# The short convolution of the heads in token-by-channel form: two partition-shifting transfers in place of transposes

## The chip, the cores and the metric

The kernel runs on one NeuronCore of a Trainium2 chip. The metric is the device time of one execution in microseconds (us). Three runs of the kernel before took 2152.03 to 2153.05 us, median 2152.1 us.

## The reference

The program is a three-layer network on 256 tokens of 2048 channels. Only the first layer matters here, and of it the attention branch. Its projection `h @ w_in` yields queries, keys and values (3 x 2048 columns), which go through a causal convolution over tokens with four taps per channel and through SiLU, before they are cut into 16 heads of 128 channels:

```python
qkv = jax.nn.silu(causal_depthwise_conv(qkv, w_conv_qkv[i]))   # frame t sees t-3..t, one weight per tap and channel
q, k, v = jnp.split(qkv, 3, axis=-1)
q, k, v = l2norm(heads(q)), l2norm(heads(k)), heads(v)
o_a = gated_delta_chunked(q, k, v, g_log, beta)
```

With x[t] the projection of token t and w0 to w3 the taps of a channel, the convolution gives w3 x[t] + w2 x[t-1] + w1 x[t-2] + w0 x[t-3]. A second convolution with 31 taps (the B branch), two attention blocks of a second network and several square projections follow.

## The kernel before

**Blocks.** All large products have the same shape: 256 tokens by 2048 inputs by 512 columns, called a block. Blocks 0 to 15 are the heads (for head h its 128 query, key, value and gate columns), blocks 16 to 31 the groups of the B branch, and 54 more follow. A block has 16 chunks of 128 input rows; each chunk is six matmuls of 512 columns (two token tiles, each three products: high weight by high input, low weight by high input, high weight by low input). The high part `w_hi` is a rounded copy of the raw weights made by ScalarE (line 436), the low part `w_lo` the difference, made by VectorE (line 443). Both engines work six chunks ahead of TensorE (`AHEAD = 6`), in buffers of eight chunks. The raw weights stand in four units of four chunks in `raw`; SyncE loads a unit of the next block when VectorE has taken the unit's last chunk (`load_heads`, four transfers of 256 KB for a unit, 16 for a block of 4 MB).

**Work beside the products.** The order on each engine is written out by hand. A block has 32 half steps, called `hs`, two for each chunk. At each half step the functions `keys_*` and `scores_*` put their own instructions between the pieces: VectorE makes one piece of `w_lo` after every odd half step, ScalarE one of `w_hi` ahead of every even one. Engines take their instructions strictly in this order. While block h+1 is multiplied, `keys_*` work on head h; `scores_*` work on head h-1 in the same block. So a head's keys are treated beside blocks 1 to 16, and its scores one block later.

**A head in `keys_*`.** At half step 0 ScalarE scales the finished sum in PSUM into `proj` (256 tokens over 128 partitions in two tiles, 512 columns; lines 530 and 531) and frees the PSUM pair. At 3 TensorE turns the query, key and value columns of `proj` into channel-by-token form in PSUM (six transposes, line 516). At 4 VectorE copies them to `conv_in` (lines 593, 594), which has three zero columns on the left. ScalarE does tap 0 at 5 (line 540), VectorE taps 1 to 3 at 7, 10 and 13 (nine instructions at line 599): in this form a tap is a shifted read along the row and its weight one number for each partition (`cw`, staged by GpSimd from `chan`). Tanh at 14 (line 544), SiLU at 16 (line 608), six transposes back at 19 (line 522), two copies to `tok` at 20 (lines 548, 549), squares at 21 (line 557). GpSimd then makes the norms (`rn`, `scal`, lines 574 to 583).

**A head in `scores_*`.** Scaling at half step 1, decay at 3 and 6, transposes of the scaled tiles at 6 (line 618), copies at 7, products of keys and queries at 9 (line 624), `ap` at 11 (line 675), stores of `ap` and `ex` to HBM at 16 from ScalarE's queue (lines 643, 644).

**Start.** `chan` is filled with channel vectors that are turned by TensorE in block 0, in eight tiles (`ROW_TILES`), two of which carry the short convolution's weights.

**Groups.** Beside blocks 17 to 32 run the 31 taps of the B branch, partly on GpSimd (line 1036, `acc_p`) with VectorE's part at line 1067. `b_buffers_pool` zeroes this stage's buffers, before the first head.

## Time and profile before

| | |
|---|---|
| median of the runs | 2152.1 us |
| the profiled execution | 2152.86 us |
| its span, first to last instruction | 2151.1 us |
| TensorE matmul busy | 2125.1 us, 99% |
| VectorE busy | 1483.1 us, 69% |
| ScalarE busy | 1240.9 us, 58% |
| GpSimd busy | 336.9 us, 16% |
| moved by DMA | 439.71 MB, mean 204 GB/s |
| granted TensorE clock, mean | 0.998 |

The page gives for each engine its busy time, then the chain of work that ended last, the costliest groups of instructions and the DMA queues. Matmuls are pipelined, so that a busy TensorE means that it was never without one, not that it was at its peak. The heads' stage is the part from about 48 to 445 us of the span; the questions about it are asked of ten blocks in its middle, from 103.72 to 350.79 us.

### The profile page before, as it was taken

What the parts mean: (1) busy time and instruction counts of PE and PEld (TensorE: products, weight loads), DVE (VectorE), ACT (ScalarE), POOL (GpSimd) and SP (SyncE); (2) the same over time, 40 slices, a digit from 0 to 9 for tenths busy, and PEclk for the clock granted to TensorE, in tenths of its full rate; (3) what the DMA queues carried; (4) which work ended last, traced back from release to release, by engine and by line L of the source; (5) the groups of instructions that cost most, each with busy time, mean ns of one, the idle gap of its engine ahead of it and who ended that gap; (6) DMA issues with size and microseconds to landing.
All of it is one profiled execution on the core that took longest, in us unless ns stands there. A gap on an engine that the chain in (4) does not pass through costs nothing.

```text
span 2151.1 us, 29138 instructions
## 1 busy us (share of the span) xinstructions
PE 2125.1 (99%) x10033; PEld 1759.0 (82%) x10033; DVE 1483.1 (69%) x2750; ACT 1240.9 (58%) x2396; POOL 336.9 (16%) x456
## 2 busy tenths in 40 slices
PE   8999999999999999999999999999999999999998
PEld 6888888888888888888888877887888888888886
DVE  5877777788999987568665564643666745456666
ACT  6666666677777864457455554553454555555543
POOL 2111111147665641010000000000000000000000
PEclk9999999999999999999999999999999999999999
DMA  8777666678877866575767655564565555554452
GB/s 261 202 205 213 197 191 201 191 216 255 240 207 215 227 205 214 196 260 187 265 249 242 233 203 195 191 195 155 198 239 194 186 192 189 185 172 139 157 212 101
DMA packets 430627, 439.71 MB, mean 204 GB/s; under 512 B 27424, under 2 KB 302112, under 8 KB 428336
## 3 DMA queue, kind: packets, MB, share of 16 engines
q1 hardware_dynamic: 412640, 380.78, 57.1%
q0 software_dynamic: 7744, 35.98, 5.0%
q10 hardware_dynamic: 10128, 21.50, 2.7%
q8 instruction: 62, 1.02, 0.2%
q14 instruction: 53, 0.43, 0.1%
HBM read 410.92 MB, written 27.28 MB: 204 GB/s over the span
## 4 chain that ended last, share of the span: by engine, by line
PE 89%; DVE 7%; issue 1%; ACT 1%; POOL 0%; DVEq 0%; POOLq 0%; ACTq 0%
PE pair L462 26%; PE pair L464 26%; PE pair L463 26%; DVE w_lo L443 3%; DVE QB L1067 2%; PE QA L1510 1%; PE RA L1526 1%; PE RA L624 1%; PE QB L1595 0%; PE RA L800 0%; PE RA L1752 0%; PE RB L1752 0%; POOL acc_p L1036 0%; PE pair L484 0%; PE pair L483 0%
## 5 line engine op out<-in xcount | busy, mean ns | idle before, releaser
L443 DVE TENSOR_TENSOR w_lo<-raw,w_hi 128x512 fp32r<-128x512 f32 x1368 | 921.8, 694 | 411.6 <-ACT w_hi L436 410.9
L436 ACT ACTIVATE w_hi<-raw 128x512 fp32r<-128x512 f32 x1368 | 828.3, 625 | 465.1 <-PE pair L464 458.1
L462 PE MATMUL pair<-w_hi,in_hi 128*128 128x512 f32 x2336 | 936.5, 401 | 3.0 <-DVE in_lo L1135 2.8
L464 PE MATMUL pair<-w_hi,in_lo 128*128 128x512 f32 x2336 | 911.9, 390 | 0.0
L463 PE MATMUL pair<-w_lo,in_hi 128*128 128x512 f32 x2336 | 910.6, 390 | 0.0
L464 PEld LDWEIGHTS pair<-w_hi,in_lo 128*128 128x128 f32 x2336 | 438.8, 188 | 93.6
L462 PEld LDWEIGHTS pair<-w_hi,in_hi 128*128 128x128 f32 x2336 | 439.3, 188 | 91.3 <-DVE in_lo L1135 3.3
L463 PEld LDWEIGHTS pair<-w_lo,in_hi 128*128 128x128 f32 x2336 | 439.7, 188 | 86.5 <-issue 1.0
L1036 POOL TENSOR_TENSOR acc_p<-acc_p,tap 128x256 f32<-128x256 f32 x160 | 184.4, 1152 | 38.5 <-ACT tap L1010 25.1
L1010 ACT ACTIVATE tap<-upad,cwl 128x256 f32<-128x256 f32 x192 | 96.9, 508 | 51.9 <-POOL acc_p L1036 51.0
L1067 DVE SCALAR_TENSOR_TENSOR QB<-upad,cwl,QB 128x256 f32<-128x256 f32 x272 | 120.0, 482 | 0.0
L599 DVE SCALAR_TENSOR_TENSOR conv<-conv_in,cw,conv 128x256 f32<-128x256 f32 x144 | 61.2, 481 | 7.4 <-ACT conv L540 7.4
L574 POOL TENSOR_TENSOR rn<-ssq,pool_eps 128x4 f32<-128x4 f32 x16 | 3.2, 201 | 335.6 <-ACT junk L557 335.6
L2139 POOL DMA_DIRECT2D ln_vec_a<-in_ln_g_dram x1 | 0.5, 533 | 350.5 <-DVE mo L1724 350.5
L462 PE MATMUL pair<-w_hi,mem_hi 128*128 128x512 f32 x128 | 52.0, 406 | 0.0
L462 PE MATMUL pair<-w_hi,oa_hi 128*128 128x512 f32 x128 | 50.8, 397 | 0.0
L462 PE MATMUL pair<-w_hi,ub_hi 128*128 128x512 f32 x128 | 50.8, 397 | 0.0
L464 PE MATMUL pair<-w_hi,mem_lo 128*128 128x512 f32 x128 | 50.0, 391 | 0.0
L464 PE MATMUL pair<-w_hi,ub_lo 128*128 128x512 f32 x128 | 49.9, 390 | 0.0
L463 PE MATMUL pair<-w_lo,mem_hi 128*128 128x512 f32 x128 | 49.9, 390 | 0.0
L463 PE MATMUL pair<-w_lo,oa_hi 128*128 128x512 f32 x128 | 49.8, 389 | 0.0
L464 PE MATMUL pair<-w_hi,oa_lo 128*128 128x512 f32 x128 | 49.8, 389 | 0.0
(440 smaller groups left out, 1902.8 us busy)
## 6 DMA issues: line engine op xcount, KB each, us to landing
raw<-in_w_in_dram SPq DMA_DIRECT2D x512, 256.0 KB, 3.9
raw<-in_w_in_dram SPq DMA_DIRECT2D x80, 1024.0 KB, 5.1
raw<-in_w_out_dram SPq DMA_DIRECT2D x48, 1024.0 KB, 5.0
raw<-in_w_kv_shared_dram SPq DMA_DIRECT2D x24, 1024.0 KB, 5.0
raw<-in_w_br_a_dram SPq DMA_DIRECT2D x16, 1024.0 KB, 5.2
raw<-in_w_br_b_dram SPq DMA_DIRECT2D x16, 1024.0 KB, 6.1
raw<-in_w_mem_kv_dram SPq DMA_DIRECT2D x16, 1024.0 KB, 4.9
raw<-in_w_ple_gate_dram SPq DMA_DIRECT2D x16, 1024.0 KB, 5.0
```

The lines of the kernel that those rows point to most:

```text
L436: act.activation(piece(blk, q)[0], raw[:, u, q % UK], ACT.Copy).then_inc(hi_ready[u], 1)
L443: dve.tensor_tensor(lo, raw[:, u, q % UK], hi.bitcast(F32), ALU.subtract).then_inc(lo_ready[u], 1)
L462: pe.matmul(o, xh, wh, start=(q == 0), stop=False)
L463: pe.matmul(o, xh, wl, start=False, stop=False)
L464: mm = pe.matmul(o, xl, wh, start=False, stop=(q == KC - 1))
L599: ins = dve.scalar_tensor_tensor(conv[:, c], conv_in[:, c, k:k + S], cw[:, k, c:c + 1], conv[:, c], ALU.mult, ALU.add)
L624: mm = pe.matmul(RA[:, tile * S:(tile + 1) * S], kq[:, 2], kq[:, 0:2].rearrange("p c n -> p (c n)"), start=True, stop=True)
L1010: act.activation(tap[:, n % 2], upad[:, par, k:k + S], ACT.Copy, scale=cwl[:, k:k + 1])\
L1036: pool.tensor_tensor(acc_p[:, :], tap[:, 0] if n == 1 else acc_p[:, :], tap[:, n % 2], ALU.add)\
L1067: dve.scalar_tensor_tensor(a, src, cwl[:, k:k + 1], a, ALU.mult, ALU.add).then_inc(long_tap[k % 2], 1)
L1510: mm = pe.matmul(QA[:, tile * P:(tile + 1) * P], probT[:, at + key * P:at + (key + 1) * P], v(key), start=(key == 0), stop=(key == n - 1))
L1526: mm = pe.matmul(RA[:, at:at + keys], q[:, tile * P:(tile + 1) * P], k[:, 0:keys], start=True, stop=True)
```

## The change

The convolution of a head stays in token-by-channel form. The taps become products of whole tiles of 128 partitions by 768 elements (two token tiles of 384 columns) with weights that are the same in all partitions. The sum is split as w3 x + w2 x1 + shift by two of (w1 x + w0 x1), where x1 is x shifted by one token. A shift by n tokens is a shift by n partitions, done by two transfers from SBUF to SBUF on ScalarE's queue: one of 128-n partitions for both tiles, and one of n partitions from the end of tile 0 to the head of tile 1. The weights of a head are loaded by SyncE as broadcast rows, 4 x 384 numbers into each of 128 partitions (768 KB), double buffered. The 12 transposes of a head, the two copies out of PSUM, the tap on ScalarE, the nine of VectorE and the two copies into `tok` are gone. GpSimd gets three instructions of 128 x 768 for each head. The half steps of `scores_*` move back by three to five, some waits of the B branch's start move (its buffers are zeroed after the last head, the first `bg` load waits for the last head's `tok`), and SyncE's loop over the heads is unrolled.

```diff
+    def taps_in_sp(sp, h, par):
+        sp.dma_start(wt[:, par], t["w_conv_qkv"][0].rearrange("k (c m) -> k c m", c=3)[:, :, bass.ds(h * P, P)].partition_broadcast(P))\
+          .then_inc(s[f"wt_in{par}"], 16)
+
+    def shift_act(act, to, src, n, done):
+        act.dma_start(to[n:P, :, :], src[0:P - n, :, 0:QKV]).then_inc(done, 16)
+        act.dma_start(to[0:n, 1], src[P - n:P, 0, 0:QKV]).then_inc(done, 16)
 
     def keys_act(act, h, par, hs):
         if hs == 0:
             act.wait_ge(psum_ready, h + 1 + BLK_A)
-            reach(act, s["qkv_cols"], h)
+            reach(act, s["one_in"], 32 * h)
             reach(act, s["z_gated"], h)
+            reach(act, s["taps_on_dve"], 4 * h - 3)
+            reach(act, s["taps_on_pool"], 3 * h - 2)
...
         if hs == 1:
             act.wait_ge(psum_free, BLK_A + h + 1)
...
+            shift_act(act, by_one, proj, 1, s["one_in"])
             act.activation(z_th[:, :, :], proj[:, :, 3 * P:4 * P], ACT.Tanh, scale=0.5).then_inc(s["z_tanh"], 1)
-        if hs == 5:
...
         if hs == 14:
-            act.wait_ge(tap_done, SHORT * h + SHORT)
-            act.activation(conv_th[:, :, :], conv[:, :, :], ACT.Tanh, scale=0.5).then_inc(s["conv_tanh"], 1)
-        if hs == 20:
...
-        if hs == 21:
+            act.wait_ge(s["taps_on_dve"], 4 * h + 3)
+            shift_act(act, by_two, qkv_old, 2, s["two_in"])
+        if hs == 24:
+            act.wait_ge(s["taps_on_dve"], 4 * h + 4)
+            reach(act, s["tok_ready"], h)
+            act.activation(qkv_th[:, :, :], qkv_sum[:, :, :], ACT.Tanh, scale=0.5).then_inc(s["conv_tanh"], 1)
+        if hs == 28:
             act.wait_ge(s["tok_ready"], h + 1)
...
     def keys_pool(pool, h, par):
+        pool.wait_ge(psum_free, BLK_A + h + 1)
+        pool.wait_ge(s[f"wt_in{par}"], 8 * h + (16 - 8 * par))
+        reach(pool, s["taps_on_dve"], 4 * h)
+        pool.tensor_tensor(qkv_new[:, :, :], proj[:, :, 0:QKV], weight(par, 3), ALU.mult).then_inc(s["taps_on_pool"], 1)
         reach(pool, s["decay_diff"], h - 1)
         reach(pool, s["tok_scaled"], h - 1)
...
+        pool.wait_ge(s["one_in"], 32 * h + 32)
+        pool.tensor_tensor(qkv_tap[:, :, :], by_one[:, :, :], weight(par, 2), ALU.mult).then_inc(s["taps_on_pool"], 1)
+        pool.wait_ge(s["taps_on_pool"], 3 * h + 2)
+        pool.tensor_tensor(qkv_new[:, :, :], qkv_new[:, :, :], qkv_tap[:, :, :], ALU.add).then_inc(s["taps_on_pool"], 1)
...
     def keys_dve(dve, h, par, hs):
-        if hs == 4:
...
-        if hs in (7, 10, 13):
...
+        if hs == 3:
+            dve.wait_ge(psum_free, BLK_A + h + 1)
+            dve.wait_ge(s[f"wt_in{par}"], 8 * h + (16 - 8 * par))
+            reach(dve, s["two_in"], 32 * h)
+            dve.tensor_tensor(qkv_old[:, :, :], proj[:, :, 0:QKV], weight(par, 1), ALU.mult).then_inc(s["taps_on_dve"], 1)
+        if hs == 11:
+            dve.wait_ge(s["one_in"], 32 * h + 32)
+            reach(dve, s["tok_ready"], h)
+            dve.tensor_tensor(qkv_sum[:, :, :], by_one[:, :, :], weight(par, 0), ALU.mult).then_inc(s["taps_on_dve"], 1)
         if hs == 12:
+            dve.wait_ge(s["taps_on_dve"], 4 * h + 2)
+            dve.tensor_tensor(qkv_old[:, :, :], qkv_old[:, :, :], qkv_sum[:, :, :], ALU.add).then_inc(s["taps_on_dve"], 1)
...
-        if hs == 16:
+        if hs == 23:
+            dve.wait_ge(s["two_in"], 32 * h + 32)
+            dve.wait_ge(s["taps_on_pool"], 3 * h + 3)
+            dve.wait_ge(s["taps_on_dve"], 4 * h + 3)
+            dve.tensor_tensor(qkv_sum[:, :, :], qkv_new[:, :, :], by_two[:, :, :], ALU.add).then_inc(s["taps_on_dve"], 1)
+        if hs == 26:
             dve.wait_ge(s["conv_tanh"], h + 1)
-            dve.scalar_tensor_tensor(conv[:, :, :], conv_th[:, :, :], 1.0, conv[:, :, :], ALU.add, ALU.mult)\
...
+            dve.scalar_tensor_tensor(tok[:, :, :, :].rearrange("p t c n -> p t (c n)"), qkv_th[:, :, :], 1.0, qkv_sum[:, :, :],
+                                     ALU.add, ALU.mult).then_inc(s["tok_ready"], 1)
...
     def group_sp(sp, j):
+        if j == 0:
+            sp.wait_ge(s["tok_ready"], HEADS)
...
-        with sp.Fori(2, HEADS) as h:
+        for h in range(2):
+            taps_in_sp(sp, h, h)
+        for h in range(2, HEADS):
             load_heads(sp, BLK_A + h, COL_A, h)
+            sp.wait_ge(s["taps_on_dve"], 4 * h - 6)
+            sp.wait_ge(s["taps_on_pool"], 3 * h - 4)
+            taps_in_sp(sp, h, h % 2)
```

In `scores_*` the scaling goes from half step 1 to 6, the transposes from 6 to 10, the copies from 7 to 11, the products from 9 to 13, `ap` from 11 to 15 and the stores from 16 to 19.

## Rows read from the trace of the kernel before

**Rows 1.** The chain that ended last, in time: start us, us, what; two neighbouring blocks

```profile
103.72 0.86 PE RA L624 x4
128.43 0.86 PE RA L624 x4
```

**Rows 2.** Ten blocks: length; PE, PEld, DVE, ACT, POOL busy (instructions); clock, DMA share, GB/s

```profile
103.72:350.79 247.07, 247.07 (x1182) 206.03 (x1181) 193.42 (x431) 161.77 (x360) 32.81 (x80) 1.00 0.69 199
```

**Rows 3.** Who VectorE waited for in these ten blocks: total us, times, longest

```profile
DVE w_lo L443 <- ACT w_hi L436: 40.1, 30, 3.2
```

**Rows 4.** TensorE's instructions in time around six transposes: start us, us

```profile
61.63 0.39 PE L464 MATMUL pair<-w_hi,in_lo 128*128 128x512 f32 x1
61.86 0.49 PE L522 MATMUL QA<-const,conv 128*128 128x128 f32 x3
...
62.75 0.40 PE L463 MATMUL pair<-w_lo,in_hi 128*128 128x512 f32 x1
62.98 0.39 PE L464 MATMUL pair<-w_hi,in_lo 128*128 128x512 f32 x1
```

**Rows 5.** VectorE's groups in the ten blocks: count, busy us, mean ns, idle before

```profile
L599 DVE SCALAR_TENSOR_TENSOR conv<-conv_in,cw,conv 128x256 f32<-128x256 f32 x90 | 38.2, 481 | 4.4 <-ACT conv L540 4.4
L608 DVE SCALAR_TENSOR_TENSOR conv<-conv_th,conv 128x768 f32<-128x768 f32 x10 | 9.5, 953 | 0.0
L593 DVE COPY conv_in<-QA 128x512 f32<-128x512 f32 x10 | 6.9, 693 | 2.1 <-PE QB L516 2.1
L675 DVE TENSOR_TENSOR ap<-RA,dexp 128x512 f32<-128x512 f32 x10 | 6.9, 686 | 0.0
L594 DVE COPY conv_in<-QB 128x256 f32<-128x256 f32 x10 | 4.1, 415 | 0.0
```

**Rows 6.** VectorE in time: three taps, then two pieces

```profile
224.91 1.28 DVE L599 SCALAR_TENSOR_TENSOR conv<-conv_in,cw,conv 128x256 f32<-128x256 f32 x3 [0.45 <-ACT conv L540]
226.10 1.29 DVE L443 TENSOR_TENSOR w_lo<-raw,w_hi 128x512 fp32r<-128x512 f32 x2
```

**Rows 7.** GpSimd's instructions in time: small one in the heads, the groups' sum alone and twice

```profile
213.22 0.20 POOL L574 TENSOR_TENSOR rn<-ssq,pool_eps 128x4 f32<-128x4 f32 x1 [21.15 <-ACT junk L557]
...
454.72 0.74 POOL L1036 TENSOR_TENSOR acc_p<-acc_p,tap 128x256 f32<-128x256 f32 x1 [0.69 <-ACT tap L1010]
...
576.40 2.38 POOL L1036 TENSOR_TENSOR acc_p<-acc_p,tap 128x256 f32<-128x256 f32 x2 [0.16 <-POOL acc_p L1036]
```

**Rows 8.** VectorE in the same stretch: two pieces beside the second of these sums

```profile
577.34 1.98 DVE L443 TENSOR_TENSOR w_lo<-raw,w_hi 128x512 fp32r<-128x512 f32 x2
```

**Rows 9.** ScalarE's groups in the ten blocks: those that the change removes

```profile
L540 ACT ACTIVATE conv<-conv_in,cw 128x256 f32<-128x256 f32 x30 | 13.1, 500 | 8.9 <-DVE conv_in L594 8.9
...
L548 ACT ACTIVATE tok<-QA 128x384 f32<-128x384 f32 x10 | 4.9, 491 | 13.2 <-PE QB L522 13.2
```

**Rows 10.** Queues and issues in the ten blocks: packets, MB, share of 16 engines; us to landing

```profile
q1 hardware_dynamic: 84477, 41.95, 61.9%
q10 hardware_dynamic: 2880, 7.21, 7.3%
values_of_heads<-ex ACTq DMA_DIRECT2D x10, 448.0 KB, 6.0
scores_of_heads<-ap ACTq DMA_DIRECT2D x10, 256.0 KB, 4.6
```

**Rows 11.** ScalarE in time: the two evictions of a head and the tanh after them

```profile
219.13 0.69 ACT L530 ACTIVATE proj<-pair,small 128x512 f32<-128x512 f32 x1 [0.73 <-PE pair L464]
220.43 0.42 ACT L534 ACTIVATE z_th<-proj 128x256 f32<-128x256 f32 x1
```

**Rows 12.** Two issues of the whole execution: KB each, median us to landing

```profile
conv_and_gate<-ubz ACTq DMA_DIRECT2D x16, 256.0 KB, 2.2
bg<-in_b_gate_dram SPq DMA_DIRECT2D x16, 64.0 KB, 4.3
```

**Rows 13.** One of ScalarE's issues of a block, in time: start us, us

```profile
206.72 0.33 ACTq L643 DMA_DIRECT2D scores_of_heads<-ap  x1
```

128 lines of the change are left out of this document (53 added, 75 removed).

## The prediction

> **What bounds the kernel now.** I read the chain of waits first. In the heads' stage it is all TensorE, and the same matmuls come back after 24.71 us [rows 1]: the period of a block. The busy times of ten blocks agree: TensorE 247.07 of 247.07 us at a granted clock of 1.00, the higher of its two levels; VectorE 193.42, 19.3 us a block; ScalarE 161.77, 16.2 a block; GpSimd 3.3 a block; DMA at 0.69 of its sixteen engines [rows 2]. VectorE idles 5.4 us a block, of which 4.0 us is waiting for ScalarE's high pieces [rows 3], which wait for free buffers. So the stage is TensorE's, with VectorE next (78%) and the DMA engines at 69%, and six chunks of lead between the pieces and the matmuls. Whatever goes from TensorE here shortens the block, until something else needs more than what is left. The change touches 16 blocks, those in which a head's keys are treated; the rest of the time stays.
>
> **What goes from TensorE.** Twelve transposes a head. Around six of them the last matmul before starts at 61.63 and the second after at 62.75 [rows 4]: 1.12 us, where two steps of 0.23 would be 0.45. So six cost 0.67 us, twelve 1.33 us, and TensorE alone would need 24.71 - 1.33 = 23.4 us a block; over 16 blocks 21.3 us less. Clock and matmuls stay as they are.
>
> **VectorE.** Gone: two copies, 0.69 and 0.42 us [rows 5], about 0.95 with their overlap, and nine taps, of which three take 1.19 us from start to next start [rows 6], so 3.6 us. Added: four products or sums of 128 x 768. SiLU has that shape and takes 0.95 us [rows 5], 0.87 without the overlap: 3.5 us. SiLU stays. 19.3 - 4.55 + 3.5 = 18.3 us a block.
>
> **GpSimd.** Added: three sums or products of 128 x 768. The trace has 0.20 us for 4 elements and 0.74 us for 256, both with two inputs [rows 7]; the line through them gives 1.84 us for 768 (bounds 0.95, VectorE's time, and 3 x 0.74 = 2.2). Three are 5.5 us. GpSimd has the room, but it does not work beside VectorE for nothing: where a sum on GpSimd runs beside two pieces of `w_lo`, two sums take 2.38 us instead of 1.48 [rows 7] and the two pieces 1.98 us instead of 1.29 [rows 8, 6]. One waits for the other. So each of the three may hold VectorE for up to 1.84 us when its next instruction reads two tiles of SBUF (pieces, taps, SiLU): 0 to 5.5 us a block. The Trainium skill ("SBUF — State Buffer", section "SBUF: two separate sides") has this as an exclusive lock held for a whole instruction, between a GpSimd instruction and a VectorE one with two SBUF inputs; the trace agrees, with the 0.69 us that the two pieces lose.
>
> **ScalarE.** Gone: three taps (13.1 us in ten blocks) and two copies to `tok` (4.9 us for one of them [rows 9]), together 2.3 us a block; added: four issues. It stays below 16 us, and is hidden.
>
> **The transfers, in engine time.** In the ten blocks (3953 us of engine time over sixteen) the load queue took 61.9% for 84477 packets, 29 ns each at a mean of 497 bytes, and ScalarE's queue 7.3% for 2880, 100 ns each at 2504 bytes [rows 10]. By the line through these two a packet of 1536 bytes (384 columns) takes 66 ns. Per block and engine today: loads 15.3 us, stores 1.8 us. The weight rows add 1536 packets of 512 bytes, 96 an engine: 2.8 us. The first shift is 127 partitions by two tiles, 254 packets; the second 252; the small transfers of one and two partitions are negligible.
>
> **How many engines carry a shift** decides the case, and no row shows it: each transfer of the hardware queues in the profile has 128, 32 or 16 rows. Bounds: all sixteen take an equal share (16 x 66 ns = 1.05 us of engine time each), or one engine takes all: 254 x 66 ns = 16.8 us. I take one engine for the first shift, because 127 rows have no equal division but 1 and 127; the second shift's 126 rows divide by 14, so 18 packets or 1.2 us each. Then that one engine has 15.3 + 1.8 + 2.8 + 16.8 + 1.2 = 37.9 us of work a block, where the block now takes 24.7. And since every weight load has a sixteenth part on each engine, the loads cannot go round it.
> The Trainium skill ("DMA: Bandwidth & Descriptors", section "Why a DMA increments its semaphore by 16 and not by 1") states such a rule: a DMA runs on the largest number up to 16 that divides the slowest dimension of both sides, so 127 partitions on one engine. No run here shows it yet; with it the sum would be the one below, without it that of the first rival.
>
> **The path through a block, with one engine.** From the end of the block's matmuls:
> - evictions until the next instruction, 1.3 us [rows 11], then the shift is issued;
> - fixed time of a transfer: one of 256 KB lands after 2.2 us [rows 12], of which 16 KB an engine at 2504 bytes in 100 ns are 0.65: 1.5 us;
> - the 254 packets, 16.8 us;
> - loads on the same engine in between: each unit has 128 packets there, 3.7 us. One unit or two fall into this time, by packets in turn at most about as many as the shift's own, so 3.7 to 7.4 us, 10.2 with the weight rows. I take 7.4, since the engine has work left over from the block before (37.9 us).
> `one_in` is reached at 27.0 us. Queued behind this wait on VectorE (half step 11) are the pieces from chunk 11 on, so TensorE stands still after chunk 10, at about 15 us. After the wait: a product 0.87, then a piece 0.6; TensorE needs 6 x 0.227 = 1.36 us for each of the chunks 11 to 15 [rows 4] and 0.9 for the scores' products [rows 1]: 9.2 us if nothing else holds it. The sum at half step 12 (0.87), `zs` (0.42, like a copy of 256 elements), `ap` (0.69) [rows 5] and four more pieces lie beside that. GpSimd's second product is released by the same semaphore, and its sum follows at once: up to 2 x 1.84 us in which VectorE stands, and late pieces then cost TensorE up to 4.2 us. So 9.2 to 13.4 us; I take 12, near the upper end since both engines start together. Period: 27.0 + 12.0 = 39.0 us, which is above the engine's own 37.9 us, so both hold.
>
> The second shift (`two_in`, awaited at half step 23) is issued after the sum at half step 12 and needs 3 to 5 us; behind it are pieces of the next block, for which TensorE has not yet come. It is late next, if the first shift were not. SyncE waits for the taps of two heads before, and its queue holds `load_heads` of the next head behind that; these taps are long done, so nothing. Unrolling its loop: nothing.
>
> **Around the stage.** Two tiles less in `ROW_TILES` spare two small transposes and copies in block 0, some 0.5 us. The first `bg` waits for the last `tok` (half step 26) and then lands in 4.3 us [rows 12], about when half step 0 of the next block wants it: 0 to 2 us once, inside the six chunks of lead. I put the sum of these at nothing, bounds -1 and +3.
>
> **Sum.** 16 x (39.0 - 24.7) = 229 us. The profiled execution took 2152.9 us (span 2151.1), 0.8 above the median of 2152.1: 2152.9 + 229 - 0.8 = 2381 us.
>
> **Rivals.**
> - *The shift is spread over all sixteen engines* (the other side). Then a shift of 390 KB lands like the 448 KB store, in 6.0 us [rows 10]: `one_in` at 7.3 us, wanted at half step 11 or 8.0 us; `two_in` at 16.3, wanted at 16.8. DMA work is 15.3 + 1.8 + 2.8 + 2.1 = 22.0 us of 23.4, nearly full. TensorE's 23.4 us against VectorE's 18.3 + up to 5.5 = 23.8: period 23.4 to 24.1, 16 x -1.3 to -0.6 us: 2131 to 2143, say 2137 us. It decides from about five engines on: with 16.8/5 = 3.4 us `one_in` comes at 8 us. For it: only the even spread of all that the profile shows. Against it: 127. Chance 0.10.
> - *Spread, but VectorE and full DMA engines take the gain back.* VectorE's locks at their upper end (3 x 2.2) give 18.3 + 6.6 = 24.9 us a block, waits for late shifts a little more: 2150 to 2165 us. Chance 0.04.
> - *One engine, and ScalarE is held too.* For it: nothing in the rows; they have the 0.33 us that an issue takes now, with packets spread evenly [rows 13]. Chance 0.06.
> - Forecast, one engine: 0.80.
>
> **How the numbers follow.** Forecast's own bounds: the path with 3.7 us of loads between and no locks is 32.5 us, but the engine's own work keeps it at 34 at least even with packets a tenth cheaper: 2301 us. With 10.2 us between and 13.4 after, 43.2 us: 2449 us. The range reaches to the third rival: 2300 to 2480, which leaves out the spread cases (0.14) and a little. What a measurement of this kernel can tell from no change is about 0.2%, 4 us. Faster 0.10, same 0.02, slower 0.88.
>
> **What would show it.** In the profile after: blocks of 36 to 43 us in the heads' stage and unchanged ones behind; VectorE idle before the product of `qkv_sum` and GpSimd before that of `qkv_tap`, some 10 us a block, ended by a DMA; the shift's issue landing after 20 us and more, that of the second after 3 to 6; mean DMA share in the stage below 0.6 although more is moved. Wrong would be: landings of 6 us and blocks under 24.7 us (first rival); ScalarE's issues several us long (last). If the engine count is right and the size wrong, the terms to look at are the loads between the packets and the 12 us after the wait.

## The result, and the profile after

| | median, us | runs from to | ratio to before, 95% interval |
|---|---|---|---|
| before | 2152.1 | | |
| after | 2587.6 | 2584.0 to 2591.3 | 1.2023 [1.2007, 1.2039] |

Predicted were 2381 us, with a range of 2300 to 2480. The change costs 435 us, where I had 229. The stage is the one predicted, the size is not: a block of the heads' stage takes more than twice its former time. The profiled execution has a span of 2583.8 us and a mean granted TensorE clock of 0.913. Over the whole run TensorE is busy 2142.7 us against 2125.1: it has hardly more to do, it waits.

The chain of waits on the page of after, shares of the span by engine:

```profile
PE 59%; DMA 22%; DVE 10%; issue 3%; ACT 3%; ACTq 2%; POOL 0%; DVEq 0%; POOLq 0%
```

A transfer, which had no share in the chain before, now has 22%. The same chain in order of time, one block of after (start us, us, what), where the chain of before held TensorE alone [rows 1]:

```profile
524.97 0.72 ACTq L526
525.69 0.03 issue
525.72 36.15 DMA by_one<-proj
...
565.02 2.61 DVE qkv_old L608
567.65 0.83 ACTq L526
...
568.51 3.85 DMA by_two<-qkv_old
...
579.14 0.72 ACTq L526
...
579.89 33.45 DMA by_one<-proj
```

The first shift takes 36 us, the second 4, and 17 us lie between the first's landing and the next head's issue. The period is 54.2 us; over the stage, from the first issue at 48.2 to the sixteenth at 839.7, it is 52.8 us on average, against 24.7 [rows 1]. Fifteen times the difference are 421 of the 435 us.

Windows of after: thirteen blocks, one block, and the stretch in it in which TensorE stands (columns as in [rows 2]):

```profile
145.00:823.00 678.00, 332.04 (x1378) 272.13 (x1378) 278.88 (x469) 175.16 (x403) 115.59 (x131) 0.73 0.51 125
523.70:577.50 53.80, 24.04 (x103) 19.71 (x103) 21.08 (x37) 13.08 (x32) 8.56 (x11) 0.71 0.54 120
532.00:560.00 28.00, 0.90 (x4) 0.91 (x5) 6.02 (x18) 3.43 (x7) 0.00 (x0) 0.50 0.38 88
```

TensorE's work in a block is 24.0 us (23.4 were expected), in a block of 53.8. While it stands, the granted clock falls to 0.50, its lower level. The DMA engines carry 125 GB/s where they carried 199 [rows 2]. Nothing is busy: everybody waits. Who waits for whom in these thirteen blocks of after (total us, times, longest):

```profile
POOL qkv_tap L574 <- DMA by_one<-proj: 458.9, 14, 34.9
DVE z L595 <- ACT z_th L545: 354.3, 13, 29.9
PE RA L633 <- DVE ex L672: 346.0, 13, 29.8
ACT z_th L545 <- issue: 343.5, 13, 29.1
```

Read from the bottom: ScalarE's tanh of z waits 26 us a block for nothing but ScalarE's own queue; VectorE's `z` waits for that tanh; the scaled rows of the scores stand behind `z` on VectorE, and TensorE's transposes wait for them. So TensorE stands not at the place I gave (a late piece behind `one_in`) but earlier, at the scores. What holds ScalarE is seen in the rows of the tile `by_one` (duration of an issue in ns, min/median/max):

```profile
L526 ACTq DMA_DIRECT2D by_one<-proj x16: 717/727/1324, 48.2 to 839.7; - x16
L527 ACTq DMA_DIRECT2D by_one<-proj x16: 9940/25228/31187, 49.5 to 840.4; - x16
```

The issue of the 127 rows is done in 0.7 us, against 0.33 for an evenly spread one [rows 13]. The next issue, of one row, takes 25 us in the median. And the weights land late (issues of these thirteen blocks: KB each, median us to landing):

```profile
raw<-in_w_in_dram SPq DMA_DIRECT2D x208, 256.0 KB, 4.1
wt<-in_w_conv_qkv_dram SPq DMA_DIRECT2D x13, 768.0 KB, 22.6
```

768 KB in 22.6 us are 35 GB/s. The single packets in the trace of after show what moves in that block, in bins of 4 us (the weights were issued at 519.6, the shift at 525.0):

```
from us | shift packets of 1536 B | packets of 512 B (weights and loads) | mean ns of one of 512 B
521     |  0                      | 1163                                 |  48
525     |  0                      |  318                                 | 166
529     |  0                      |  290                                 | 116
533     |  0                      |  340                                 |  39
537     |  0                      |  463                                 |  82
541     | 43                      | 1656                                 |  31
545     | 48                      |  155                                 |  27
549     | 47                      |   46                                 |  27
553     | 57                      |   21                                 |  27
557     | 58                      | 1870                                 |  29
```

For 16 us after the shift's issue none of its packets moves; about 80 packets of 512 bytes a microsecond do at first, 41 GB/s. At about 541 the weights are in, the loads that had piled up pass (1656 packets in 4 us), and the shift's packets start, one each 75 ns or so, 65 ns of it its own time. They come one after another, all 254 of them, at least 60 ns apart; in the reordered kernel below, where the shift is cut at row 112, more than ten are under way at once. This is how one engine by itself would carry them.

### The profile page after: what moved, and what is told of

Its sections match the earlier page's. It is cut to its first block, busy times and chain, and to the rows that moved or that the text cites. A ratio compares the mean times of both kernels' runs of the same rounds, so it can differ in the third digit from the quotient of the medians.

```text
span 2583.8 us, 28297 instructions
## 1 busy us (share of the span) xinstructions
PE 2142.7 (83%) x9839; PEld 1766.9 (68%) x9839; DVE 1516.6 (59%) x2636; ACT 1197.7 (46%) x2316; POOL 426.8 (17%) x487
## 4 chain that ended last, share of the span: by engine, by line
PE 59%; DMA 22%; DVE 10%; issue 3%; ACT 3%; ACTq 2%; POOL 0%; DVEq 0%; POOLq 0%
DMA by_one<-proj 20%; PE pair L469 17%; PE pair L471 17%; PE pair L470 17%; DVE w_lo L450 3%; DMA by_two<-qkv_old 2%; DVE qkv_old L608 2%; DVE QB L1084 1%; ACTq L526 1%; ACTq L527 1%; ACT w_hi L443 1%; ACT junk L559 1%; PE QA L1530 1%; PE RA L1546 1%; DVE tok L623 1%
## 5 line engine op out<-in xcount | busy, mean ns | idle before, releaser
L450 DVE TENSOR_TENSOR w_lo<-raw,w_hi 128x512 fp32r<-128x512 f32 x1368 | 946.5, 711 | 362.6 <-ACT w_hi L443 360.5
L443 ACT ACTIVATE w_hi<-raw 128x512 fp32r<-128x512 f32 x1368 | 819.0, 625 | 515.7 <-PE pair L471 464.7
L633 PE MATMUL RA<-const,scaled 128*128 128x128 f32 x48 | 14.1, 429 | 385.9 <-DVE ex L672 385.9
L633 PEld LDWEIGHTS RA<-const,scaled 128*128 128x128 f32 x48 | 7.9, 208 | 392.6 <-DVE ex L672 225.5
L595 DVE SCALAR_TENSOR_TENSOR z<-z_th,proj 128x256 f32<-128x256 f32 x16 | 6.8, 425 | 429.7 <-ACT z_th L545 429.7
L545 ACT ACTIVATE z_th<-proj 128x256 f32<-128x256 f32 x16 | 6.7, 416 | 415.7 <-issue 415.7
L574 POOL TENSOR_TENSOR qkv_tap<-by_one,wt 128x768 f32<-128x768 f32 x16 | 41.5, 2594 | 495.0 <-DMA by_one<-proj 495.0
```

The costliest lines, as they stand in the source:

```text
L443: act.activation(piece(blk, q)[0], raw[:, u, q % UK], ACT.Copy).then_inc(hi_ready[u], 1)
L450: dve.tensor_tensor(lo, raw[:, u, q % UK], hi.bitcast(F32), ALU.subtract).then_inc(lo_ready[u], 1)
L574: pool.tensor_tensor(qkv_tap[:, :, :], by_one[:, :, :], weight(par, 2), ALU.mult).then_inc(s["taps_on_pool"], 1)
```

## The experiments

All on the changed kernel, with the kernel before on the same chip. The period is the average over the stage: from the first issue of `by_one` to the sixteenth, by fifteen.

| kernel | median, us | ratio to before, 95% interval | period, us |
|---|---|---|---|
| after | 2587.6 | 1.2023 [1.2007, 1.2039] | 52.8 |
| shift in 112 + 15 rows | 2375.2 | 1.1033 [1.1014, 1.1051] | 39.1 |
| two weight loads in all | 2380.4 | 1.1081 [1.1043, 1.1118] | 39.1 |
| small transfer first | 2635.1 | 1.2225 [1.2165, 1.2286] | 56.4 |
| 112 + 15 rows and two weight loads | 2273.6 | 1.0561 [1.0543, 1.0579] | 32.6 |
| 112 + 15 rows, distinct weight rows | 2252.2 | 1.0465 [1.0447, 1.0482] | 30.8 |
| 112 + 15 rows, weights by tap | 2387.9 | 1.1098 [1.1079, 1.1116] | 40.0 |
| scores later | 2271.4 | 1.0547 [1.0523, 1.0570] | 32.1 |
| distinct rows, narrow GpSimd | 2169.1 | 1.0082 [1.0065, 1.0099] | 25.7 |
| distinct rows, reordered | 2153.5 | 1.0005 [0.9996, 1.0015] | 24.6 |
| sixteen copies, reordered | 2181.2 | 1.0135 [1.0118, 1.0152] | 26.7 |
| the same, copies early | 2177.7 | 1.0110 [1.0093, 1.0126] | 26.5 |
| the same, shift in 127 rows | 2432.2 | 1.1300 [1.1281, 1.1319] | 42.2 |

### The shift cut at row 112

```diff
-        act.dma_start(to[n:P, :, :], src[0:P - n, :, 0:QKV]).then_inc(done, 16)
+        act.dma_start(to[n:n + 112, :, :], src[0:112, :, 0:QKV]).then_inc(done, 16)
+        act.dma_start(to[n + 112:P, :, :], src[112:P - n, :, 0:QKV]).then_inc(done, 16)
```

> The changed kernel with each large shift cut in two transfers of 112 rows (16 times 7) and of the 15 or 14 rows left, same bytes and same result; the small transfers stay. Theory A (127 rows ride on one DMA engine, and the weight rows' slow load, 20 us of packets on every engine, stands before them): the engine count no longer matters, the shift's packets take about 1 us an engine; if packets of the two queues take turns, one_in lands some 6 to 8 us after its issue and blocks come back after 24 us (about 2145 us); if the shift waits for the whole weight load, it lands after some 15 to 18 us and ScalarE's hold shrinks, blocks of 30 to 35 us (2240 to 2320 us). Theory B (a shift between partitions of SBUF is slow by itself, however it is spread): landing stays above 30 us, time stays near 2590 us.

Measured 2375.2 us: with the slow weight loads in place the one engine costs 212 of the 435 us, and 223 are left. The shift no longer needs 17 us of one engine, and still lands after 17.5 us (issues from 200 to 400 us: KB, us to landing):

```profile
wt<-in_w_conv_qkv_dram SPq DMA_DIRECT2D x5, 768.0 KB, 22.6
by_one<-proj ACTq DMA_DIRECT2D x5, 336.0 KB, 17.5
```

The weights land after 22.6 us here as in after, and the shift lands when they do. That is above the 2320 us at which the expectation ended: I had not thought that a spread shift would wait for the whole weight load.

### Weights for two heads only

```diff
-            taps_in_sp(sp, h, h % 2)
```

> The changed kernel without the weight loads of heads 2 to 15: these heads use the weight rows of heads 0 and 1, so that the load of 768 KB a head is left out; the shifts stay as they are. Theory A: the first packet of the shift comes 1.5 to 2 us after its issue instead of 15 to 16, the transfer of 254 packets lands after 19 to 25 us, ScalarE's second issue is held 10 to 16 us instead of 25 to 28; blocks of 36 to 40 us instead of 52, 2330 to 2400 us. Theory B, and a third one (C) by which the order of descriptors within ScalarE's queue and not the weight load delays the shift: no change, near 2590 us.

Measured 2380.4 us, as expected. Without loads of weights in its way the 127-row shift lands after 19 us (the chain in time), and the next issue is held 10 us instead of 25:

```profile
299.65 18.72 DMA by_one<-proj
...
336.66 19.00 DMA by_one<-proj
```

```profile
L527 ACTq DMA_DIRECT2D by_one<-proj x16: 10004/10690/34067, 49.5 to 634.8; - x16
```

So of the 25 us that ScalarE is held in after, about 15 are the time in which the weights block the shift, and 10 the one engine's. That this time is the predicted one is chance. The prediction had the weight rows in it, at 2.8 us, and two of its terms are off in opposite directions here: from TensorE's last matmul of a block to the landing it takes 21.4 us (334.28 to 355.66), where the prediction had 27.0, and from the landing to the block's last matmul 15.9 us (318.37 to 334.28), where it had 12.

### The small transfer first

```diff
-        act.dma_start(to[n:P, :, :], src[0:P - n, :, 0:QKV]).then_inc(done, 16)
         act.dma_start(to[0:n, 1], src[P - n:P, 0, 0:QKV]).then_inc(done, 16)
+        act.dma_start(to[n:P, :, :], src[0:P - n, :, 0:QKV]).then_inc(done, 16)
```

> The changed kernel with the two transfers of a shift issued in the other order, the one of one or two rows first; nothing else. Theory A (ScalarE is not held by the 127 rows' own issue but by the next issue behind it, until all but about a hundred of the 254 packets are through): ScalarE goes on at once, z_th and the high pieces follow, TensorE gets through chunk 10 instead of standing after chunk 4, while one_in comes as late as before (34 to 37 us after the issue). The block shrinks by the 6 chunks of 1.36 us and the 5 us from z_th to scaled, 52 to 41 or 45 us: 2410 to 2480 us. Rival (the hold is that of the large transfer's own issue, or TensorE waits for one_in anyway): 2570 to 2600 us.

Measured 2635.1 us, a miss on the wrong side. The held issue did go: ScalarE's two issues take 0.6 and 2.7 us in the median. But other instructions wait now, as long as before (waits from 200 to 400 us):

```profile
POOL qkv_tap L574 <- DMA by_one<-proj: 143.8, 4, 37.6
ACT w_hi L443 <- issue: 131.1, 8, 33.7
DVE qkv_sum L605 <- DMA by_one<-proj: 110.4, 4, 28.5
```

ScalarE's high pieces wait up to 33.7 us, but not for a held issue. In ScalarE's program the second shift's issue comes at half step 14, and ahead of it the wait for VectorE's sum, which needs the landed shift. The high pieces behind stand there too. One block in time, VectorE's sum and that issue, then the block's last matmul (the thirtieth after TensorE's stand, five chunks) and the eviction behind it:

```profile
330.62 2.58 DVE L608 TENSOR_TENSOR qkv_old<-qkv_old,qkv_sum 128x768 f32<-128x768 f32 x1
333.23 0.66 ACTq L526 DMA_DIRECT2D by_two<-qkv_old  x1
...
341.87 0.39 PE L471 MATMUL pair<-w_hi,in_lo 128*128 128x512 f32 x1
...
343.81 0.67 ACT L536 ACTIVATE proj<-pair,small 128x512 f32<-128x512 f32 x1
```

TensorE gets through chunk 10 before it stands, as expected, and has five chunks left at the landing (327.5) instead of eleven. It doesn't help, for two reasons. It comes out of a stand of 19.3 us at the lower clock level and needs 11.5 us for these five chunks. And the next head's shift is not issued when TensorE is through, but when the second shift (4.9 us), the last sum, SiLU and the squares are done, which stand ahead of the evictions in ScalarE's program: the eviction comes 1.5 us after the last matmul's end, 0.5 us in after. From the landing to the next shift's issue it takes 18.1 us here (272.40 to 290.52) and 17.3 in after. So the hold lies beside the wait for the shift and this chain: taking it away gives nothing while the shift takes 36 us. What makes the block 3.6 us longer than in after is not settled; the two landings shown by the chain take 38.0 and 36.4 us, against 36.2 and 33.5.

### Both: 112 + 15 rows, weights for two heads

> Both edits of the first two: shifts of 112 and 15 (14) rows, and no weight loads for heads 2 to 15 (these heads use the weights of heads 0 and 1). Theory A: what is left is the arithmetic of the change; one_in lands after 5 to 7 us, TensorE is never without work in the heads' stage or VectorE, locked by GpSimd's three instructions, is just as slow: blocks of 23.4 to 24.7 us, 2131 to 2152 us. If VectorE's and GpSimd's contention costs more than its measured durations say: 25 to 28 us a block, 2160 to 2205 us. Theory B: above 2500 us.

Measured 2273.6 us. A shift (its 336 KB) now lands after 3.1 us in the median, and 121 us over the kernel before remain, above both expectations. With the two runs before it makes a square:

| | weights each head | weights of two heads |
|---|---|---|
| shift in 127 rows | 2587.6 | 2380.4 |
| shift in 112 + 15 rows | 2375.2 | 2273.6 |

The weight loads cost 207 us beside the slow shift and 102 beside the fast one; the one engine costs 212 with the loads and 107 without. Together they cost more (314 us) than the two alone added up (209), though the landings nearly add (3.1, 17.5, 19 and 36 us): with a landing of 3.1 us the block of 32.6 us is bound by something else, and the first delay uses up part of that time. The third part, 121 us, is neither. About 21 of it are the weights of the first two heads, which are still loaded slowly (see the distinct rows below). The rest has its rows here, from the waits and from VectorE in time, 200 to 400 us:

```profile
PE RA L634 <- DVE ex L673: 34.1, 7, 5.0
DVE z L596 <- ACT z_th L546: 28.6, 7, 4.1
```

```profile
233.37 0.42 DVE L596 SCALAR_TENSOR_TENSOR z<-z_th,proj 128x256 f32<-128x256 f32 x1 [4.08 <-ACT z_th L546]
...
236.52 3.77 DVE L670 TENSOR_SCALAR scaled<-tok,scal 128x128 f32<-128x128 f32 x3
...
240.40 0.67 DVE L670 TENSOR_SCALAR scaled<-tok,scal 128x128 f32<-128x128 f32 x3
```

TensorE waits up to 5 us in each block for the scaled rows. Before these VectorE stands 4.1 us for the tanh of z, which is queued behind three issues on ScalarE (0.71, 0.91 and 0.61 us), and then three scalings take 3.77 us that take 0.67 elsewhere.

### Scores four half steps later

```diff
-        if hs == 10:
+        if hs == 14:
```

This is TensorE's wait for the scaled rows; likewise the copies, products and `ap`, and the tanh ahead of the issues; otherwise as the run before.

> The kernel of e4_both (even shifts, weight loads for heads 0 and 1 only) with two shifts of order: ScalarE does the gate's tanh before it issues the first shift, and the transposes, copies, products, ap and stores of scores_* come four half steps later on every engine. Theory F (in e4_both TensorE idles 5 us a block in front of the scores' transposes, because VectorE is late with scaled, and then runs some 4 us at the lower clock): both go, blocks of 23.4 to 25 us, 2135 to 2160 us. Rival G (VectorE and GpSimd are together full, and the idle time only moves to the pieces of w_lo): 2230 to 2275 us.

Measured 2271.4 us; it moved nothing (2273.6 before). The wait found another place: the copies of the scores, now at half step 15, stand on ScalarE behind half step 14, where it waits for VectorE's sum and then issues the second shift (waits, 200 to 400 us).

```profile
ACT kq L652 <- issue: 58.4, 7, 8.4
PE RA L640 <- ACT ex L653: 26.0, 7, 3.8
```

VectorE's three scalings still take 3.86 us beside GpSimd in this run, and its sum, which ScalarE waits for, comes behind them. The theory that the scores were only placed too early fell with this run. The time is in the range of its rival, that VectorE and GpSimd are together full, but the run leaves GpSimd's work as it is and can't show that.

### What makes the weight load slow: distinct rows

The same 1536 packets of 512 bytes to the same partitions, but each partition reads rows of its own of `w_in` and not all 128 the same 6 KB. Shift in 112 + 15 rows.

```diff
-        sp.dma_start(wt[:, par], t["w_conv_qkv"][0].rearrange("k (c m) -> k c m", c=3)[:, :, bass.ds(h * P, P)].partition_broadcast(P))\
+        sp.dma_start(wt[:, par].rearrange("p k c m -> p (k c) m"), w_in[:, 0, 0:12 * 1408].rearrange("p (g m) -> p g m", g=12)[:, :, bass.ds(h * 64, P)])\
```

> The kernel of e1_rows112 with another source for the weight rows: 1536 pieces of 512 bytes a head as before, but each partition reads twelve pieces of its own row of w_in instead of the same twelve pieces of w_conv_qkv as all others (so the taps are wrong numbers). Theory D (the weight load is slow, 23 us for 768 KB at 80 packets a us, because 128 partitions read the same 6 KB of HBM, and all other packets stand behind it): landing 4 to 8 us, shifts of 2.5 to 4 us, time near that of e4_both, 2270 to 2300 us. Theory E (it is slow by its size, its number of pieces or the shape of the access, whatever it reads): landing stays at 20 to 25 us and the time near e1_rows112's 2375 us.

Measured 2252.2 us, against 2375.2 with the broadcast. The landings (200 to 400 us):

```profile
wt<-in_w_in_dram SPq DMA_DIRECT2D x6, 768.0 KB, 6.1
by_one<-proj ACTq DMA_DIRECT2D x7, 336.0 KB, 3.1
```

22.6 us have become 6.1 for the same bytes, packets and destination, and the shift's 17.5 have become 3.1. So it is neither the volume nor the 512-byte packets. It is that one stretch of HBM is read by all partitions, and what ScalarE's queue has to move waits meanwhile. (The tensor read is another one too, but `w_conv_qkv` is not slow by itself: where distinct stretches of it are read, in the copying of the run with sixteen copies further down, 96 KB in pieces of 512 bytes land after 2.6 us.) The time is even 21 us below that of the kernel without loads: the first two heads' weights came sooner too (waits for them 19.8 us over all engines, 40.9 there).

### Weights in four transfers, one a tap

```diff
-        sp.dma_start(wt[:, par], t["w_conv_qkv"][0].rearrange("k (c m) -> k c m", c=3)[:, :, bass.ds(h * P, P)].partition_broadcast(P))\
+        for k in range(SHORT):
+            sp.dma_start(wt[:, par, k], t["w_conv_qkv"][0].rearrange("k (c m) -> k c m", c=3)[k, :, bass.ds(h * P, P)].partition_broadcast(P))\
```

> The kernel of e1_rows112 with the weight rows of a head in four transfers of 192 KB, one for each tap, instead of one of 768 KB; same bytes, same result. Theory D (same HBM bytes for all partitions): each of the four goes at the same slow rate, 5 to 6 us each, 20 us in all, and the shift of ScalarE's queue waits for those already handed over; 2340 to 2380 us. Theory E in its form 'the one large transfer keeps the others out until it has ended': the shift gets in between two of the four, lands after 4 to 9 us, 2290 to 2330 us.

Measured 2387.9 us, 13 us above the run with one transfer and 8 above the expected range. Four shorter transfers let nothing through between them: the shift still lands after 18.1 us in the median. The slow load is not a matter of the size of one transfer.

### GpSimd's three instructions made narrow

```diff
-        pool.tensor_tensor(qkv_tap[:, :, :], by_one[:, :, :], weight(par, 2), ALU.mult)
+        pool.tensor_tensor(qkv_tap[:, :, 0:4], by_one[:, :, 0:4], weight(par, 2)[:, :, 0:4], ALU.mult)
```

and likewise the other two, on the kernel with distinct rows.

> As the run with distinct weight rows (2252.2 us), and GpSimd's three instructions of a head work on 4 of their 768 columns only; so the current token and the token one back are left out of the sum, and the sum of the older two taps takes their place. GpSimd's 5 to 8 us of 768-column work per head, during which VectorE's instructions there were longer (3.8 us for the scaled rows against 2.1), are gone; VectorE's own work and all transfers stay. Theory G, what is left over the kernel before (100 us, 6.2 per block) is for the most part VectorE standing while GpSimd works: 3 to 5 us per block come back, 2170 to 2205 us, and the idle time of TensorE before the scores' transposes (79 us in the whole run) falls to under 40. Theory H, it is VectorE's own work and the wait for the shifts: GpSimd's instructions lie beside it and the time stays at 2235 to 2255 us.

Measured 2169.1 us, 83 us less than 2252.2, and 1 us below the range of the theory that VectorE stands for GpSimd. In the kernel with distinct rows, VectorE and GpSimd in time:

```profile
330.63 2.34 DVE L450 TENSOR_TENSOR w_lo<-raw,w_hi 128x512 fp32r<-128x512 f32 x1
332.89 2.02 DVE L687 TENSOR_TENSOR dexp<-dexp,const 128x256 f32<-128x256 f32 x1
334.84 0.68 DVE L450 TENSOR_TENSOR w_lo<-raw,w_hi 128x512 fp32r<-128x512 f32 x1
335.44 0.66 DVE L670 TENSOR_SCALAR scaled<-tok,scal 128x128 f32<-128x128 f32 x3
```

```profile
330.22 2.20 POOL L575 TENSOR_TENSOR qkv_tap<-by_one,wt 128x768 f32<-128x768 f32 x1 [1.79 <-DMA by_one<-proj]
332.50 2.13 POOL L577 TENSOR_TENSOR qkv_new<-qkv_new,qkv_tap 128x768 f32<-128x768 f32 x1
```

A piece of `w_lo` takes 2.34 us instead of 0.68, and `dexp` 2.02 instead of 0.42, each until 0.3 to 0.6 us after the end of a GpSimd instruction. Together they put the scaled rows 3.3 us later. The two instructions of GpSimd are released by `one_in`, so they come just then: the faster the shift, the earlier in the block they fall, ahead of the scores. This is why a shift of 3.1 us did not bring the time back.
With narrow instructions TensorE's wait for the scaled rows falls, and the clock stays at its higher level; the waits from 145 to 400 us, first with distinct rows, then with the narrow instructions:

```profile
PE RA L634 <- DVE ex L673: 44.8, 9, 5.0
```

```profile
PE RA L634 <- DVE ex L673: 17.4, 10, 1.8
```

From 145 to 640 us this idle time is 64.7 us with wide instructions and 20.7 with narrow ones, where the expectation said under 40. Over the whole profile TensorE's idle time falls by 52 us (108.8 to 56.6) and its busy time by 30 (2140.2 to 2110.4), for the same matmuls. The 30 go with the clock: with waits of 5 us a block its mean from 200 to 400 us is 0.89, with waits of 1.8 it is 1.00. The Trainium skill ("SBUF — State Buffer", section "SBUF: two separate sides") has the lock between GpSimd and a VectorE instruction with two SBUF inputs as one for the whole instruction; the 2.34 and 2.02 us agree with that. In the kernel with both edits the scalings, which have one input, took 3.77 us beside GpSimd.

### Reordered

Nothing left out but the true weights (distinct rows again). The tanh of z comes ahead of the first shift's issue, the issue moves to half step 4, and GpSimd waits for the scaled rows before its wide instructions:

```diff
+            act.activation(z_th[:, :, :], proj[:, :, 3 * P:4 * P], ACT.Tanh, scale=0.5).then_inc(s["z_tanh"], 1)
+        if hs == 4:
...
             shift_act(act, by_one, proj, 1, s["one_in"])
-            act.activation(z_th[:, :, :], proj[:, :, 3 * P:4 * P], ACT.Tanh, scale=0.5).then_inc(s["z_tanh"], 1)
...
         reach(pool, s["taps_on_dve"], 4 * h)
+        reach(pool, s["tok_scaled"], h)
         pool.tensor_tensor(qkv_new[:, :, :], proj[:, :, 0:QKV], weight(par, 3), ALU.mult).then_inc(s["taps_on_pool"], 1)
```

> As the run with distinct weight rows (2252.2 us), with three things moved and nothing left out: the gate's tanh runs ahead of the shift's issue in ScalarE's program, the first shift is issued three half steps later (after the half step's evictions), and GpSimd waits with its three 768-column instructions until VectorE has written the scaled rows of the scores before. Theory G (VectorE stands while GpSimd works): the scaled rows come 1.5 to 2 us sooner, TensorE's idle time before the scores' transposes falls from 79 us to under 50 in the whole run, and the time to 2190 to 2225 us. Theory H: 2240 to 2260 us, the later GpSimd work only puts the last sum later.

Measured 2153.5 us (2149.3 to 2157.1), no difference from before, and 99 us less than in the old order: more than I had expected of it. The three moves were made together, so the share of each is open. The window from 200 to 400 us, and TensorE's neighbours in the waits of that stretch:

```profile
200.00:400.00 200.00, 198.19 (x894) 162.24 (x893) 187.07 (x310) 117.49 (x263) 110.76 (x86) 1.00 0.94 273
```

```profile
POOL qkv_new L571 <- DVE ex L675: 47.2, 9, 5.2
DVE z L598 <- ACT z_th L541: 7.4, 9, 0.8
```

TensorE works all the time again, at the higher clock level, and the period in the middle of the stage is 23.9 us (GpSimd's first small sum starts at 318.57 and again at 342.43), below the 24.7 of before. GpSimd and VectorE lose no less to each other than they did, but where six chunks of lead cover it:

```profile
326.30 6.05 POOL L571 TENSOR_TENSOR qkv_new<-proj,wt 128x768 f32<-128x768 f32 x1 [5.24 <-DVE ex L675]
```

1.84 us of work take 6.05 here. VectorE is busy 187 of 200 us and the DMA engines 94%. So little more could come from the order: the block gains 0.8 us, about 12 us over the stage, which the first heads, whose weights are late, eat up (TensorE is busy 133.8 of the 140 us from 60 to 200, against 140.0 before).

### The whole computation with sixteen copies of the weights

```diff
+        for i in range(16):
+            sp.dma_start(taps_dram[i].rearrange("h (q m) -> h q m", m=P), t["w_conv_qkv"][0].rearrange("k (c h m) -> h (k c) m", c=3, m=P))\
+              .then_inc(s["out_stored"], 16)
...
-        sp.dma_start(wt[:, par], t["w_conv_qkv"][0].rearrange("k (c m) -> k c m", c=3)[:, :, bass.ds(h * P, P)].partition_broadcast(P))\
+        for g in range(P // 16):
+            sp.dma_start(wt[16 * g:16 * g + 16, par].rearrange("p k c m -> p (k c m)"), taps_dram[:, bass.ds(h, 1), :].rearrange("i a n -> i (a n)"))\
```

> The changed kernel whole, with nothing left out: shifts cut at row 112, the order of the run before, and the weights read in each head from sixteen copies in HBM that the kernel makes at its start (each of the 16 copies is read by 8 partitions in place of one 6 KB stretch by 128; 16 times 98 KB of copying ahead of the first head). Theory D, it is the 128 readers of one stretch that make the weight load slow: its landing falls from 22.7 us to under 12, and the time is that of the run before plus at most 20 us, 2200 to 2250 us. If eight readers of one stretch are slow too, the landing stays over 15 us and the time at 2300 to 2375 us.

Measured 2181.2 us, 406 us less than after, 1.35% above before, and below the expected 2200 to 2250 us. Each transfer of sixteen partitions lands after 4.3 us in the median, as the reading of the slow load wants it: eight readers of one stretch are not slow.

With the copies issued between the raw loads of the second block and the first head's weights ahead of the decays' transfers:

> As the run with sixteen copies (2181.2 us), nothing left out: the copies are issued one after each raw load of the second block (not in a row behind them), and the first head's weights ahead of the decays' two transfers. In the run before, the engines waited 43.6 us for the weights of the first two heads and TensorE was busy 120.4 of the 140 us from 60 to 200, against 133.8 in the run with distinct rows. Expected: those waits fall by 10 to 25 us, and with them the time to 2155 to 2172 us; the block of the ten middle heads stays. If it stays at 2178 to 2184 us, the first heads were not on the path.

Measured 2177.7 us (2172.2 to 2178.8), hardly less, a miss. The waits for the first weights did fall (from 43.6 to 23.7 us over all engines), but the middle of the stage got no better (window from 200 to 400 us):

```profile
200.00:400.00 200.00, 186.65 (x822) 153.13 (x821) 168.47 (x286) 106.95 (x245) 74.95 (x78) 0.97 0.95 256
```

The DMA engines are at 95% there, carrying 256 GB/s instead of the 273 of the reordered kernel. The shift lands after 4.8 us in place of 3.1. So 24 us over the reordered kernel stay; they go with the DMA engines, which are full in both, but that is argued and not shown; which property of the copied loads makes them dearer (6 KB in one piece, eight issues a head, eight readers) was not tried. No version that computes the whole beats the kernel before.

### The one engine by itself

The kernel of the run before, with the shifts in 127 and 126 rows again.

> As the run before of this call, with one thing put back: each shift again in 127 and 126 rows, so that the 127 rows of the first go to one engine. It is the price of the one engine alone, with the weights landing in about 5 us and GpSimd's work after the scaled rows. By the sum of the prediction: first packet about 2 us after the issue, 254 packets of 1536 B at 65 ns on one engine, 16.8 us, and that engine's share of the loads between (up to 7 us), so a landing of 19 to 26 us in place of 3 to 5; issue at the fourth half step, 5 to 6 us into the block, and some 14 us after the landing: a block of 38 to 46 us, 2385 to 2500 us in all. Against it, that the one engine takes less than the sum, because it drains while nothing else moves: 2300 to 2385 us. Were the one engine of no weight, and the slow weight load all of it, the time would be within 20 us of the run before.

Measured 2432.2 us, in the expected range: 254 us, 15.9 a block, for the one engine alone. The chain in time and the issues:

```profile
313.21 22.17 DMA by_one<-proj
...
354.74 21.63 DMA by_one<-proj
```

```profile
L530 ACTq DMA_DIRECT2D by_one<-proj x16: 722/724/1320, 50.1 to 683.8; - x16
L531 ACTq DMA_DIRECT2D by_one<-proj x16: 12126/14098/24087, 51.5 to 684.5; - x16
```

A landing 22 us after the second issue, 22.4 and 22.9 after the first, within the 19 to 26 of the sum, where the cut shift takes 5.

## Why the prediction missed, point by point

- *What bounds the kernel, and what goes from TensorE.* Right. In the reordered kernel, where nothing else is late, the block takes 23.9 us; the prediction had 23.4 for TensorE alone. Of the 1.3 us a block of the transposes 0.8 were gained.
- *How many engines carry a shift.* Right: one packet after the other, 65 ns each (predicted 66), for 254 packets; and the cut into 112 rows, which is 16 times 7, brings 212 us in after and 254 in the last pair. The rule of the Trainium skill ("DMA: Bandwidth & Descriptors", section "Why a DMA increments its semaphore by 16 and not by 1"), by which 127 rows go to one engine, agrees with a landing of 19 us against 3.1. The forecast's chance was well placed there; its price was not the only one.
- *The transfers, weight rows at 2.8 us an engine.* This step failed, and it is the largest part. I priced the broadcast by packets (1536 at 29 ns, over sixteen engines). It took 22.6 us, and nothing of the shift moved meanwhile. From the last matmul of a block to the landing it takes 39.3 us in after (522.54 to 561.87), where the prediction had 27.0, and without these loads 207 us of the 435 go. The row that should have warned me was in [rows 12]: a broadcast of 64 KB lands after 4.3 us, and a store of 256 KB in 2.2; twelve times that, for 768 KB, would be 52 us (34 without the fixed 1.5), and I used that row for `bg` alone.
- *The loads in between, 3.7 to 7.4 us, by packets in turn.* Wrong twice. While the weights came, there was no taking turns: no packet of the shift in 16 us. After them the loads that had piled up were through in 4 us, and for the 12 us after that hardly any was left, since TensorE stood and the buffers were full. Without weight loads the whole landing is 19.8 us from the issue, so the loads cost about 1.5 over the 18.3 of the other terms; with fast ones it is 22.4 to 22.9, so they cost 4.1 to 4.6. The Trainium skill ("DMA: Bandwidth & Descriptors", section "Queues, rings and completion order") has each DMA engine taking turns between the queues, one packet at a time, where a packet is typically 9 to 17 descriptors and 64 at most. A packet of this profile is one piece of 512 bytes, and the weights have 96 of them for an engine (1536 by sixteen). That none of the shift's moved for 16 us does not agree with turns of 9 to 17 pieces; whether turns of 64 would give it, no run here tells.
- *After `one_in`, 12 us.* This step failed too, by 3.5 us a block: from the landing to the block's last matmul it takes 15.5 us in after (561.87 to 577.33) and 15.9 without weight loads. Two wide GpSimd instructions of 2.60 and 2.18 us and, beside them, a piece of 2.31 and a sum of 2.60 us on VectorE are in the prediction's upper end. Not in it: TensorE comes out of 30 us of standing at the lower clock level and runs its first matmuls at 0.43 us each instead of 0.23, and it has eleven chunks left, not five. Nor is the other path in it, which the prediction put at nothing ("behind it are pieces of the next block"): second shift, last sum, SiLU and squares, ahead of the evictions on ScalarE. It is the one that the chain of after shows; the eviction comes at 577.87, 0.5 us after the last matmul's end, so the two paths end together here, and where TensorE had less left (small transfer first) this one alone kept the next shift back.
- *ScalarE.* "Four issues, hidden" was wrong, the third rival was right about the mechanism: a queue takes 127 rows for one engine only in part, and the rest holds ScalarE, 25 us in after, 10 to 14 where the weights are fast. It comes at the issue after the long one. I gave it 0.06, since nothing in the rows spoke for it. Its price was wrong all the same: it lies beside the wait for the shift and the chain behind it, as the run with the small transfer first shows, and moved only the place where TensorE stands.
- *GpSimd's locks, 0 to 5.5 us a block.* In the sum I let them count after `one_in` only. They are real there, but their largest price shows when the shift is fast: 83 us, 5.2 a block.
- *The first rival* (sixteen engines give 2137 us) was wrong as well. The shift did land after 3.1 us, faster than its 6.0, and the kernel still took 2273.6 us without weight loads. Its sum had TensorE against VectorE's total and no look at which instruction is late: the tanh behind three issues, and the scaled rows behind GpSimd. It comes true, to 16 us, only with these moved.
- *Around the stage.* The first head waits for its weights, 26.6 us on GpSimd in after; I had put these at nothing.
- *The range* was built of the price of one mechanism. The unknown cost of the broadcast had no upper bound in it, though no row showed a transfer of such a source and size.

By the runs the 435 us are: 207 for the broadcast in the presence of the one engine (102 without it), 107 for the one engine without it, and 121 for the rest. Of these about 21 are the broadcasts of the first two heads, and 100 the order and the locks, of which the reordered kernel gets back 99 with distinct rows. What the locks alone cost is shown with the narrow instructions, 83 us.

## What to carry to other kernels

Price a transfer by its source as well as by its bytes and packets: a load that gives all partitions the same few kilobytes of HBM took 3.7 times as long as one of distinct rows, and held the packets of ScalarE's queue up. Cut a shift over partitions so that its longest transfer has a multiple of 16 rows; the rest may be a second transfer. Follow what waits for a late transfer to the next issue of the same kind, over every engine and its written order, and not over the engine that bounds the kernel alone. And before moving wide work to GpSimd, look at what VectorE does at the moment of its release: the same instructions cost 5.2 us a block ahead of the step TensorE waits for, and nothing that the time shows in the reordered kernel, behind it.

## What the runs showed of the hardware

- A 768 KB load with the same 6 KB of HBM for 128 partitions: 22.6 us, about 80 packets of 512 bytes a microsecond. The same from distinct rows: 6.1 us. Sixteen partitions from sixteen copies, with eight such transfers at once: 4.3 us.
- 381 KB from SBUF to SBUF: 127 rows in one transfer 18.7 to 22.2 us, 112 + 15 rows 3.1 to 4.9 us (17.5 behind the slow load). 126 rows, in the second shift, 3.7 to 4.9 us. A packet of 1536 bytes takes 65 ns, one of 512 bytes 27.
- The issue of a 127-row transfer itself takes 0.7 us; the issue after it, if it comes at once, takes 10 us, and 25 where the transfer can't start.
- A sum of 128 x 768 on GpSimd takes 1.84 us alone, as the line through two smaller ones gave it, and up to 6.05 us where VectorE is busy with two-input instructions; a two-input VectorE instruction beside it ended 0.3 to 0.6 us after it.
- After a wait of 5.0 us on TensorE (distinct rows) the next matmuls ran at 0.43 us each, the lower clock level, and the mean granted clock from 200 to 400 us was 0.89; with waits of 1.8 us (narrow instructions) it was 1.00.
